# Two transformer blocks on one core: the filling matmuls of zeros taken out of TensorE's stream

## The chip, the cores and the metric

The kernel runs on one core of a Trainium2 chip. The metric is the device time of one execution in microseconds (us), of which the median of several runs is given; lower is better. The trace and the page come from one profiled execution.

## What is computed

256 tokens of width 1024 pass, in fp32, through three layers. The reference, cut to what matters here:

```python
# first block, two layers i = 0, 1
xn, mn = rms_norm(h, norm_mix[i]), rms_norm(mem, norm_mem[i])
# i = 0: forgetting attention, 12 heads of 64, causal, bias F[t] - F[s]
# i = 1: causal attention with ALiBi slopes, 12 heads of 64
# both: 4 more heads attend to 256 memory rows, without bias
h = h + heads @ w_out[i]
hn = rms_norm(h, norm_ffn[i])
h = h + (silu(gate) * up) @ w_down[i]
# second block, one layer
z = rms_norm(x) @ w_in
o_mla  = softmax(q @ k.T) @ v              # 16 heads, q and k 96 wide, v 64 wide
o_diff = (softmax(q1 @ k1.T) - lam * softmax(q2 @ k2.T)) @ v   # 8 heads, v 128 wide
x = x + (gate_a * o_mla + gate_b * norm(o_diff)) @ w_out
h2 = rms_norm(x)
affinity = softmax(h2 @ router_w)          # 16 experts
gate, idx = top_k(affinity per expert, 32) # each expert takes 32 tokens
y = (silu(xe @ w_gate) * (xe @ w_up)) @ w_down   # 1024 -> 2048 -> 1024 per expert
x = x + scatter_add(gate * y)
```

## The kernel before, in words

The program is written by hand, engine by engine: each engine has its own list of instructions in the order in which the code gives them, and the lists meet at semaphores (`wait_ge`, `then_inc`). Nothing reorders them, so an instruction on TensorE delays all that stand behind it there.

*Dense products.* Weights come in units of 1 MB into a ring in SBUF. ScalarE (L676) rounds a unit to its high part `wH`, VectorE (L1426) makes the low part `wL`, and TensorE multiplies high by high, high by low and low by high (`passes`, L992 to L994) into one PSUM sum. Activations are split the same way into `xH` and `xL`. This holds for the projections of both blocks, the output projections and the feed-forward loops.

*Norms.* A norm (`mem`, `mix0`, `ffn0`, `mix1`, `ffn1`, `attn`, `ffn2`, in this order) begins with squares on ScalarE (L699), a sum on VectorE, a root on ScalarE (L703) and the reciprocal, from which VectorE builds diagonal matrices (L1437). Then `transposes` on TensorE (L1014) multiplies the tokens by them and so turns and scales them at once; it waits for `norm_diag`. ScalarE and VectorE bring the result to SBUF, and the next dense product follows, column block by column block.

*Attentions.* There are four: `a0` and `a1` (layers 0 and 1 of the first block), `mla` and `dif` (second block). The first three have 32 maps (a head and a block of 128 queries each), two to a chunk, so 16 chunks; the width of a map is 128 or 256 keys for the causal heads, 256 for all others. TensorE's function `attention` goes round once per chunk: scores of chunk i (L1061, into banks 0 to 3), value products of chunk i-2 (L1075, 64 columns each), transposes of the probabilities of chunk i-1 (L1087). VectorE adds the bias (made by GpSimd, L605 and L609 in `a0`) and takes the row extreme (L1460, L1463), ScalarE takes the exponentials (L741), and VectorE copies the transposed probabilities to `pT_sb` (L1479), for which the value products wait. `dif` has a loop of its own with the same steps for 16 pairs of maps (L1313 scores, L1326 value products, L1336 transposes), in which VectorE mixes the two maps and ScalarE copies `pT_sb`. Behind each attention `turn_outputs` (L1101) transposes the outputs, and `out_proj` multiplies by the output weights.

*Matmuls of zeros.* `zeros` is a 128x512 bf16 tile, set once. `keep_busy(n, b)` (L999) issues n matmuls of it into bank b, 512 columns each; their result is never read, since the next matmul into that bank starts its sum anew. It is called:

- in `transposes`, ahead of the wait for the diagonal matrices: 30 for `attn`, 14 for `ffn0`, `mix1`, `ffn1`, `ffn2`;
- in `attention` and the loop of `dif`, behind the scores of the second and third iteration: 8 and 6 (`FILL`);
- in the same loops, ahead of the transposes of a chunk, from the third chunk on: 2 for `a0`, `mla` and `dif`, 1 for `a1` (`BUSY`), behind a wait for `att_pT`;
- 16 behind the loop of `dif`, and 18 in the choice of tokens, while VectorE looks for each expert's 32 best (L1831, L1833).

That is 86 + 56 + 98 + 34 = 274. Eight more matmuls of zeros at L1217 open the sums of the two feed-forward loops; they are not issued by `keep_busy`.

*Choice of tokens and experts.* The router product (L1129, 16 columns per matmul) is followed by a softmax, the search on VectorE, and matmuls by a 0/1 selection matrix (L1365). Then a loop over the 16 experts streams 24 MB of weights per expert through ten places of 1 MB; SyncE issues the transfers as places come free. The first places are filled while the attentions and the choice of tokens run.

Of the kernel before, what the change touches and what calls it, by code (L numbers as in the profile page):

```python
# [28 lines left out]
P = 128  # L29
# [33 lines left out]
def build(nc, x, mem, norm_mix, norm_mem, norm_ffn, norm_final, w_in_fox, b_fgate, w_in_moba,  # L63
# [4 lines left out]
    with ctx:  # L68
        def sb(name, shape, dt=F32):
            return ctx.enter_context(nc.sbuf_tensor(name, shape, dt))  # L70
# [5 lines left out]
        bank = [ctx.enter_context(nc.psum_tensor(f"bank{i}", [P, 512], F32)) for i in range(8)]  # L76

        def b2(i):
            return bank[i][:, :].rearrange("p (a n) -> p a n", a=2)
# [20 lines left out]
        zeros = sb("zeros", [P, 512], BF16)  # L100
# [122 lines left out]
        def diag(t):  # L223

            return pT_sb[:, t, 0, 0:P]
# [71 lines left out]
        def norm_at(name, k, v):  # L297

            before = NORMS.index(name) - (k == "dve")
            return before * ADDS[k] + v  # L300
# [65 lines left out]
        def width(kind, m):  # L366
            hd, qt = MAPS[m]
            return P * (qt + 1) if kind != "mla" and hd < NSELF else S

        def score_operands(kind, m):  # L370
            hd, qt = MAPS[m]
            if kind == "mla":
                return qTm[0:MLA_QK, hd, P * qt:P * qt + P], kTm[0:MLA_QK, hd, :]
            if hd < NSELF:
                return (kslice(qT, hd)[:, P * qt:P * qt + P], kslice(kT, hd)[:, 0:width(kind, m)])
            return kslice(qmT, hd - NSELF)[:, P * qt:P * qt + P], kslice(mkT[int(kind[1])], hd - NSELF)

        def value(kind, m, kt):
            hd, _ = MAPS[m]
            if kind == "mla":  # L380
                return v_mla[:, kt, HD * hd:HD * hd + HD]
            if hd < NSELF:
                return v_s[:, kt, HD * hd:HD * hd + HD]
            return v_m[int(kind[1])][:, kt, HD * (hd - NSELF):HD * (hd - NSELF) + HD]
# [36 lines left out]
        def _(sp):  # L421
# [32 lines left out]
            for n, (w, c0, _, _) in zip(mem_u[2:], MEMPROJ[2:]):  # L454
                load_cols(n, w, c0)
# [532 lines left out]
        def _(pe):  # L988
# [4 lines left out]
                pe.matmul(out, lh, rl, start=False, stop=False)  # L993
                return pe.matmul(out, ll, rh, start=False, stop=stop)  # L994

            def keep_busy(n, b):

                for _ in range(n):
                    pe.matmul(bank[b][:, :], zeros[:, 0:P], zeros[:, :], start=True, stop=True)  # L999

            def x_part(k, cols=slice(0, S)):
                return xH[:, k, cols], xL[:, k, cols]

            def transposes(name, src, first=4):

                n = nrm
                if name not in ("mem", "mix0"):
                    keep_busy(30 if name == "attn" else 14, 0)
                pe.wait_ge(n["diag"], norm_at(name, "diag", 2))
                for b in range(4):  # L1010
                    for j in range(2):
                        for t in range(NT):
                            k = 2 * b + j
                            mm = pe.matmul(b2(first + b)[:, j, P * t:P * t + P], src[:, t, P * k:P * k + P],  # L1014
                                           diag(t), start=True, stop=True)
                    mm.then_inc(n["tr"], 1)
# [29 lines left out]
                return [b2(b)[:, j, :] for j in range(2)]  # L1046


            BUSY = {"a0": 2, "a1": 1, "mla": 2, "dif": 2}

            FILL = (0, 8, 6)

            def attention(name, kind):
                base = att_base[name]
                for i in range(NMAP // 2 + 2):
                    if i < NMAP // 2:
                        if i >= 2:
                            pe.wait_ge(att["exp"], base["exp"] + 2 * i - 2)
                        for m in (2 * i, 2 * i + 1):
                            l, r = score_operands(kind, m)  # L1060
                            mm = pe.matmul(bank[m % 4][:, 0:width(kind, m)], l, r, start=True, stop=True)  # L1061
                        mm.then_inc(att["score"], 1)
                    if i < len(FILL):
                        keep_busy(FILL[i], 7)
                    if 0 <= i - 2 < NMAP // 2:
                        c = i - 2
                        g = c // 4
                        pe.wait_ge(att["pT"], base["pT"] + c + 1)
                        if c % 4 == 0 and g >= 2:
                            pe.wait_ge(att["o"], base["o"] + g - 1)  # L1070
                        for m in (2 * c, 2 * c + 1):
                            j = m % 8
                            nk = width(kind, m) // P
                            for kt in range(nk):
                                mm = pe.matmul(bank[6 + g % 2][:, HD * j:HD * j + HD],  # L1075
                                               pT_sb[:, c % 2, m % 2, P * kt:P * kt + P], value(kind, m, kt),
                                               start=(kt == 0), stop=(kt == nk - 1))
                        mm.then_inc(att["pv"], 1)
                    if 0 <= i - 1 < NMAP // 2:
                        c = i - 1  # L1080
                        if c >= 2:
                            pe.wait_ge(att["pT"], base["pT"] + c - 1)
                            keep_busy(BUSY[name], 4 + c % 2)
                        pe.wait_ge(att["exp"], base["exp"] + 2 * c + 2)
                        for m in (2 * c, 2 * c + 1):
                            for kt in range(width(kind, m) // P):
                                mm = pe.transpose(b2(4 + c % 2)[:, m % 2, P * kt:P * kt + P],  # L1087
                                                  p_sb[:, m % 4, P * kt:P * kt + P], ident[:, :])
                        mm.then_inc(att["tr"], 1)
# [55 lines left out]
            for L in range(2):  # L1145
                name = f"mix{L}"
# [10 lines left out]
                for u, (n, (_, _, how, _)) in enumerate(zip(proj_u[L], projections(L))):  # L1157
# [7 lines left out]
                    if L == 0 and u == 5:  # L1165
# [6 lines left out]
                        for i in range(6):  # L1172
                            if i >= 2:
                                pe.wait_ge(f_ev, i)
                            for j in range(2):
# [3 lines left out]
                                               start=True, stop=True)  # L1179
# [7 lines left out]
                name = f"ffn{L}"  # L1187
# [48 lines left out]
            for b in range(2):  # L1236
                for j in range(2):
                    for t in range(NT):
                        c = 2 * b + j
# [67 lines left out]
            for i in range(16 + 3):  # L1307
                if i < 16:
                    hd, qt = 4 * (i // 8) + i % 4, (i // 4) % 2
                    if i >= 2:  # L1310
                        pe.wait_ge(att["exp"], base["exp"] + 2 * i - 2)
                    for j in range(2):
                        mm = pe.matmul(bank[(2 * i + j) % 4][:, 0:S],  # L1313
                                       dqT[HD * j:HD * j + HD, hd, P * qt:P * qt + P],
                                       dkT[HD * j:HD * j + HD, hd, :], start=True, stop=True)
                    mm.then_inc(att["score"], 1)
                if i < len(FILL):
                    keep_busy(FILL[i], 7)
                if 0 <= i - 3 < 16:
                    n = i - 3  # L1320
                    hd, g, j = 4 * (n // 8) + n % 4, n // 4, n % 4
                    pe.wait_ge(att["pT"], base["pT"] + n + 1)
                    if j == 0 and g >= 2:
                        pe.wait_ge(att["o"], base["o"] + g - 1)
                    for kt in range(2):
                        mm = pe.matmul(bank[6 + g % 2][:, P * j:P * j + P], pT_sb[:, n % 2, 0, P * kt:P * kt + P],  # L1326
                                       v_d[:, kt, P * hd:P * hd + P], start=(kt == 0), stop=(kt == 1))
                    mm.then_inc(att["pv"], 1)
                if 0 <= i - 2 < 16:
                    n = i - 2  # L1330
                    if n >= 2:
                        pe.wait_ge(att["pT"], base["pT"] + n - 1)
                        keep_busy(BUSY["dif"], 4 + n % 2)
                    pe.wait_ge(dif_mix, n + 1)
                    for kt in range(2):
                        mm = pe.transpose(bank[4 + n % 2][:, P * kt:P * kt + P],  # L1336
                                          mix_sb[:, n % 2, P * kt:P * kt + P], ident[:, :])
                    mm.then_inc(att["tr"], 1)
            keep_busy(16, 4)
            turn_outputs("dif", 4, sn_mul)  # L1340
            out_proj(wout2_u, mTL, 0, 1)

# [8 lines left out]
            for t in range(NT):  # L1351
                mm = pe.transpose(bank[5][0:NE, P * t:P * t + P], aff[:, t, :], ident[:, :])
            mm.then_inc(ro_tr, 1)
            keep_busy(18, 7)
            pe.wait_ge(ro_key, 14)
            for t in range(NT):
                mm = pe.transpose(bank[6][:, NE * t:NE * t + NE], affT[:, 0, P * t:P * t + P], ident[0:NE, 0:NE])
# [4 lines left out]
            for k in range(KD):  # L1362
                for t in range(NT):
                    for part in (tokH, tokL):
                        mm = pe.matmul(bank[k][:, :], part[t][:, P * k:P * k + P],  # L1365
                                       sel[:, t].rearrange("p e c -> p (e c)"),
                                       start=(t == 0 and part is tokH), stop=(t == 1 and part is tokL))
# [3 lines left out]
            with pe.Fori(0, NE) as e:  # L1371
# [13 lines left out]
                for half in range(2):  # L1385
                    for k in range(KD):
                        w_ = arrived(8 * half + k)
                        for j in range(4):
                            mm = pe.matmul(bank[half][32 * j:32 * j + 32, :], xe[:, k, :],  # L1389
                                           w_[:, 512 * j:512 * j + 512],  # L1390
                                           start=(k == 0), stop=(k == KD - 1))
# [8 lines left out]
                for kc in range(16):  # L1400
                    if kc % 2 == 0:
                        w_ = rows_of(arrived(16 + kc // 2))
                    for q in range(4):
                        mm = pe.matmul(bank[3][32 * q:32 * q + 32, 0:256], hT[:, kc % 4, 32 * (kc // 4):32 * (kc // 4) + 32],  # L1404
                                       w_[:, kc % 2, 256 * q:256 * q + 256],
                                       start=(kc == 0), stop=(kc == 15))
# [490 lines left out]
```

## Time and profile before

| | us |
|---|---|
| median of 3 runs | 2052.25 |
| lowest and highest run | 2052.20, 2053.24 |
| span of the profiled execution, first to last instruction | 2051.5 |
| TensorE busy with matmuls | 1636.2 (80% of the span) |
| TensorE loading weights | 1064.7 (52%) |
| VectorE busy | 603.4 (29%) |
| ScalarE busy | 567.1 (28%) |
| GpSimd busy | 117.8 (6%) |
| mean granted clock of TensorE | 0.850 of full speed |
| read from HBM | 539.55 MB |

For the profiled execution the profile gives its span and no other time of its own; the runs' median lies 0.75 us above that span, which leaves that much for what lies around it. Busy times are shares of the whole span, an average over stages with different limits. The granted clock is what TensorE's throttle allowed: 1.0 is 2.4 GHz, 0.5 is 1.2 GHz, and a mean between them is a mixture of both.

### The profile page before, as it was taken

How to read it: one execution, taken by the hardware profiler on the slowest of the kernel's cores; microseconds unless marked ns; L12 is line 12 of the kernel's file. 1: busy time of each engine (PE TensorE's matmuls, PEld its weight loads, DVE VectorE, ACT ScalarE, POOL GpSimd, SP SyncE). 2: the span in 40 equal slices, each digit the busy share in tenths (PEclk: the TensorE clock that was granted, in tenths of full speed). 3: DMA queues.
4: the chain of work that ended last, by engine and by line, in shares of the span. 5: the costliest groups of instructions: out<-in, count | busy, mean ns of one | idle time of the engine just before them, and what ended most of it. 6: DMA issues, size and time to landing. Idle time of an engine off the chain costs nothing.

```text
span 2051.5 us, 27650 instructions
## 1 busy us (share of the span) xinstructions
PE 1636.2 (80%) x11433; PEld 1064.7 (52%) x11433; DVE 603.4 (29%) x867; ACT 567.1 (28%) x881; POOL 117.8 (6%) x167
## 2 busy tenths in 40 slices
PE   7999999999999998799887666666666666666666
PEld 6877999896899987789573111111111111111111
DVE  4344444545444445555752000000000000000000
ACT  6344344443543445625631000000000000000000
POOL 0040000002000003510100000000000000000000
PEclk9899999999999989999998677677677767776776
DMA  9421555450455523305144999999999999999998
GB/s 278 152 83 62 166 186 187 157 185 22 152 187 187 177 87 123 123 5 183 62 164 188 419 418 417 417 417 417 419 419 418 417 417 417 417 419 419 417 417 339
DMA packets 181999, 541.47 MB, mean 264 GB/s; under 512 B 12606, under 2 KB 106003, under 8 KB 149171
## 3 DMA queue, kind: packets, MB, share of 16 engines
q1 hardware_dynamic: 181890, 540.51, 68.8%
q8 instruction: 42, 0.69, 0.1%
q0 software_dynamic: 48, 0.13, 0.0%
q14 instruction: 19, 0.15, 0.0%
HBM read 539.55 MB, written 1.05 MB: 264 GB/s over the span
## 4 chain that ended last, share of the span: by engine, by line
PE 47%; DMA 37%; DVE 5%; ACT 4%; POOL 3%; SPq 2%; issue 2%; DVEq 0%; ACTq 0%; POOLq 0%
DMA ring<-in_expert_w_up_dram 17%; PE bank L992 11%; PE bank L993 11%; PE bank L994 11%; DMA arena<-in_expert_w_down_dram 10%; DMA ring<-in_expert_w_gate_dram 4%; PE bank L1389 4%; PE bank L1075 2%; PE bank L1129 1%; SPq L525 1%; DMA ring<-in_expert_w_down_dram 1%; PE bank L999 1%; DMA wide_L<-in_expert_w_up_dram 1%; DMA wide_H<-in_expert_w_down_dram 1%; DMA wide_L<-in_expert_w_gate_dram 1%
## 5 line engine op out<-in xcount | busy, mean ns | idle before, releaser
L1426 DVE TENSOR_TENSOR wL<-ring,wH 128x2048 fp32r<-128x2048 f32 x128 | 294.6, 2301 | 358.9 <-ACT wH L676 358.9
L676 ACT ACTIVATE wH<-ring 128x2048 fp32r<-128x2048 f32 x128 | 244.2, 1908 | 350.8 <-PE bank L994 349.2
L992 PE MATMUL bank<-xH,wH 128*128 128x256 f32 x1056 | 300.0, 284 | 4.4 <-DVE wL L1426 4.2
L993 PE MATMUL bank<-xL,wH 128*128 128x256 f32 x1056 | 298.8, 283 | 0.0
L994 PE MATMUL bank<-xH,wL 128*128 128x256 f32 x1056 | 298.7, 283 | 0.0
L1389 PE MATMUL bank<-ring,arena 128*32 128x512 f32 x1280 | 220.2, 812 | 71.8 <-DMA ring<-in_expert_w_up_dram 51.9
L992 PEld LDWEIGHTS bank<-xH,wH 128*128 128x128 f32 x1056 | 202.5, 192 | 6.7 <-issue 5.8
L993 PEld LDWEIGHTS bank<-xL,wH 128*128 128x128 f32 x1056 | 202.6, 192 | 0.8
L994 PEld LDWEIGHTS bank<-xH,wL 128*128 128x128 f32 x1056 | 202.6, 192 | 0.0
L1866 DVE TENSOR_TENSOR arena<-arena,bank 128x512 f32<-128x512 f32 x16 | 11.0, 688 | 541.4 <-PE bank L1389 541.4
L1389 PEld LDWEIGHTS bank<-ring,arena 128*32 128x32 f32 x1280 | 37.8, 132 | 244.2 <-DMA ring<-in_expert_w_up_dram 140.7
L1870 DVE TENSOR_TENSOR h<-h,bank 128x512 f32<-128x512 f32 x64 | 39.7, 682 | 348.6 <-PE bank L1413 348.6
L992 PE MATMUL bank<-wH,xH 128*128 128x256 f32 (+1 forms) x416 | 130.4, 313 | 2.5 <-DVE xL L1802 1.7
L993 PE MATMUL bank<-wL,xH 128*128 128x256 f32 (+1 forms) x416 | 129.5, 311 | 0.0
L994 PE MATMUL bank<-wH,xL 128*128 128x256 f32 (+1 forms) x416 | 129.4, 311 | 0.0
L980 ACT ACTIVATE arena<-bank 128x512 f32<-128x512 f32 x16 | 9.6, 597 | 329.3 <-PE bank L1396 329.3
L982 ACT ACTIVATE arena<-bank 128x256 f32<-128x256 f32 x16 | 6.1, 384 | 288.4 <-PE bank L1404 288.4
L992 PE MATMUL bank<-wH,hidH 128*128 128x512 f32 (+1 forms) x208 | 81.7, 393 | 5.2 <-DVE hidL L1677 2.0
L992 PEld LDWEIGHTS bank<-wH,xH 128*128 128x128 f32 x416 | 80.9, 195 | 7.5 <-issue 3.7
L994 PEld LDWEIGHTS bank<-wH,xL 128*128 128x128 f32 x416 | 80.8, 194 | 4.0
L993 PEld LDWEIGHTS bank<-wL,xH 128*128 128x128 f32 x416 | 80.8, 194 | 3.8
L993 PE MATMUL bank<-wL,hidH 128*128 128x512 f32 (+1 forms) x208 | 81.2, 391 | 0.0
(266 smaller groups left out, 2114.2 us busy)
## 6 DMA issues: line engine op xcount, KB each, us to landing
ring<-in_expert_w_gate_dram SPq DMA_DIRECT2D x96, 1024.0 KB, 19.2
ring<-in_expert_w_up_dram SPq DMA_DIRECT2D x64, 1024.0 KB, 24.2
ring<-in_w_gate_up_dram SPq DMA_DIRECT2D x44, 1024.0 KB, 5.1
arena<-in_expert_w_up_dram SPq DMA_DIRECT2D x32, 1024.0 KB, 26.0
ring<-in_expert_w_down_dram SPq DMA_DIRECT2D x32, 1024.0 KB, 27.3
wide_H<-in_expert_w_down_dram SPq DMA_DIRECT2D x32, 1024.0 KB, 20.5
wide_L<-in_expert_w_down_dram SPq DMA_DIRECT2D x32, 1024.0 KB, 18.8
arena<-in_expert_w_down_dram SPq DMA_DIRECT2D x32, 1024.0 KB, 18.7
```

What stands on the lines that cost most here:

```text
L525: sp.dma_start(dst, gv[e, u]).then_inc(landed, 16)
L676: act.activation(wH[:, n % 2, w], ring[:, slot(n), w], ACT.Copy).then_inc(w_hi, 1)
L992: pe.matmul(out, lh, rh, start=start, stop=False)
L993: pe.matmul(out, lh, rl, start=False, stop=False)
L994: return pe.matmul(out, ll, rh, start=False, stop=stop)
L999: pe.matmul(bank[b][:, :], zeros[:, 0:P], zeros[:, :], start=True, stop=True)
L1075: mm = pe.matmul(bank[6 + g % 2][:, HD * j:HD * j + HD], pT_sb[:, c % 2, m % 2, P * kt:P * kt + P], value(kind, m, kt), start=(kt == 0), s ...
L1129: mm = pe.matmul(out, l, r, start=(start and j == 0), stop=(stop and j == 1))
L1389: mm = pe.matmul(bank[half][32 * j:32 * j + 32, :], xe[:, k, :], w_[:, 512 * j:512 * j + 512], start=(k == 0), stop=(k == KD - 1))
L1426: dve.tensor_tensor(wL[:, n % 2, w], ring[:, slot(n), w], wH[:, n % 2, w].bitcast(F32), ALU.subtract).then_inc(w_split, 1)
L1866: dve.tensor_tensor(hid, sg, bank[1][:, :], ALU.mult).then_inc(e_hid, 1)
L1870: dve.tensor_tensor(hv, hv, b2(4 + q), ALU.add).then_inc(e_add, 1)
```

## The change

`keep_busy`, its tables `BUSY` and `FILL` and all of its calls are taken out; the waits around them stay. Nothing is put in their place. The tile `zeros` and the eight matmuls at L1217 remain.

```diff
@@
-            def keep_busy(n, b):
-
-                for _ in range(n):
-                    pe.matmul(bank[b][:, :], zeros[:, 0:P], zeros[:, :], start=True, stop=True)
-
@@ def transposes(name, src, first=4):
                 n = nrm
-                if name not in ("mem", "mix0"):
-                    keep_busy(30 if name == "attn" else 14, 0)
                 pe.wait_ge(n["diag"], norm_at(name, "diag", 2))
@@
-            BUSY = {"a0": 2, "a1": 1, "mla": 2, "dif": 2}
-
-            FILL = (0, 8, 6)
-
             def attention(name, kind):
@@
                         mm.then_inc(att["score"], 1)
-                    if i < len(FILL):
-                        keep_busy(FILL[i], 7)
@@
                             pe.wait_ge(att["pT"], base["pT"] + c - 1)
-                            keep_busy(BUSY[name], 4 + c % 2)
                         pe.wait_ge(att["exp"], base["exp"] + 2 * c + 2)
@@ the loop of dif
-                if i < len(FILL):
-                    keep_busy(FILL[i], 7)
@@
                         pe.wait_ge(att["pT"], base["pT"] + n - 1)
-                        keep_busy(BUSY["dif"], 4 + n % 2)
                     pe.wait_ge(dif_mix, n + 1)
@@
-            keep_busy(16, 4)
             turn_outputs("dif", 4, sn_mul)
@@ the choice of tokens
             mm.then_inc(ro_tr, 1)
-            keep_busy(18, 7)
             pe.wait_ge(ro_key, 14)
```

Because lines are taken out, L1014, L1061, L1075 and L1087 of before are L1007, L1050, L1062 and L1073 in the changed kernel. The order of instructions on VectorE, ScalarE, GpSimd and SyncE is the same in both.

TensorE in `a0`, one iteration with wide maps, before (`arena` holds queries, keys and values; `p_sb` the probabilities):

```order
L1061 MATMUL bank<-arena 128x256 [waits att_exp]
L1061 MATMUL bank<-arena 128x256
L1075 MATMUL bank<-arena,pT_sb 128x64 [waits att_pT]
L1075 MATMUL bank<-arena,pT_sb 128x64 x3
L999 MATMUL bank<-zeros 128x512 [waits att_pT]
L999 MATMUL bank<-zeros 128x512
L1087 MATMUL bank<-ident,p_sb 128x128 [waits att_exp]
L1087 MATMUL bank<-ident,p_sb 128x128 x3
```

The same iteration in the changed kernel:

```order
L1050 MATMUL bank<-arena 128x256 [waits att_exp]
L1050 MATMUL bank<-arena 128x256
L1062 MATMUL bank<-arena,pT_sb 128x64 [waits att_pT]
L1062 MATMUL bank<-arena,pT_sb 128x64 x3
L1073 MATMUL bank<-ident,p_sb 128x128 [waits att_exp,att_pT]
L1073 MATMUL bank<-ident,p_sb 128x128 x3
```

The transposes stand directly behind the value products, and the wait for `att_pT` has moved to them.

TensorE at the norm `ffn0`, between the output projection of `a0` and the first product of the feed-forward, before:

```order
L994 MATMUL bank<-wH,xL 128x512
L999 MATMUL bank<-zeros 128x512 x14
L1014 MATMUL bank<-pT_sb,h 128x128 [waits norm_diag]
L1014 MATMUL bank<-pT_sb,h 128x128 x15
L992 MATMUL bank<-xH,wH 128x256 [waits norm_dve,w_split]
```

And in the changed kernel:

```order
L994 MATMUL bank<-wH,xL 128x512
L1007 MATMUL bank<-pT_sb,h 128x128 [waits norm_diag]
L1007 MATMUL bank<-pT_sb,h 128x128 x15
L992 MATMUL bank<-xH,wH 128x256 [waits norm_dve,w_split]
```

Between the last product of the projection and the wait for the diagonal matrices nothing is left.

## Rows read from the trace of the kernel before

**Rows 1.** The page, part 2: granted clock of TensorE in 40 slices, in tenths.
```profile
PEclk9899999999999989999998677677677767776776
```

**Rows 2.** The chain that ended last, first expert: start us, us, what.
```profile
1118.70 18.81 DMA arena<-in_expert_w_down_dram
```

**Rows 3.** The tile `zeros`: matmuls, duration ns min/median/max, first and last start.
```profile
L999 PE MATMUL bank<-zeros x274: 377/379/634, 127.3 to 1088.2; 128*128 128x512 bf16 x137
```

**Rows 4.** The chain, a wide chunk of `a0`.
```profile
157.85 1.10 PE bank L1075 x8
158.96 0.43 PE bank L999 x2
159.39 0.45 PE bank L1087 x4
...
159.86 0.70 DVE pT_sb L1479
```

**Rows 5.** The attentions `a0`, `a1`, `mla`, `dif`: busy by engine, clock, DMA share, GB/s.
```profile
127.00:170.80 43.80, 39.28 (x258) 26.35 (x256) 24.12 (x81) 16.36 (x64) 26.68 (x44) 0.96 0.08 26
460.20:501.20 41.00, 36.80 (x248) 25.59 (x248) 24.24 (x81) 15.81 (x64) 14.35 (x20) 0.96 0.10 32
860.40:909.30 48.90, 46.48 (x298) 36.28 (x299) 26.08 (x56) 16.23 (x64) 0.00 (x0) 1.00 0.00 1
989.40:1030.00 40.60, 36.61 (x206) 21.69 (x207) 32.00 (x118) 24.48 (x85) 10.16 (x12) 0.94 0.05 21
```

In these rows the engines are, in order: TensorE's matmuls, its weight loads, VectorE, ScalarE, GpSimd.

**Rows 6.** The chain, GpSimd in `a0`.
```profile
139.84 0.46 POOL bias_sb L609
140.29 0.91 POOL bias_sb L605
```

**Rows 7.** The chain, `a1`: the first fill, and one matmul of zeros in a chunk.
```profile
460.89 3.01 PE bank L999 x8
...
476.58 0.22 PE bank L999
```

**Rows 8.** The chain, a chunk of `mla`.
```profile
874.34 1.02 PE bank L1075 x8
875.37 0.43 PE bank L999 x2
875.80 0.44 PE bank L1087 x4
876.23 0.87 PE bank L1061 x4
```

**Rows 9.** TensorE in time order, norms `ffn0` and `attn`; in brackets idle before and releaser.
```profile
196.08 3.20 PE L999 MATMUL bank<-zeros 128*128 128x512 bf16 x14
...
730.11 1.16 PE L1014 MATMUL bank<-pT_sb,h 128*128 128x128 f32 x8 [1.66 <-DVE pT_sb L1437]
```

**Rows 10.** The chain, the transposing matmuls of `ffn0`.
```profile
199.63 3.84 PE bank L1014 x32
```

**Rows 11.** Stretches with their granted clock (the columns of rows 5).
```profile
748.10:755.00 6.90, 6.90 (x35) 6.90 (x34) 2.04 (x6) 1.82 (x7) 0.00 (x0) 0.50 0.49 152
853.90:857.30 3.40, 3.40 (x18) 3.23 (x17) 0.00 (x0) 2.05 (x3) 3.40 (x2) 0.50 0.65 224
857.30:860.70 3.40, 2.16 (x18) 1.88 (x17) 0.00 (x0) 2.98 (x5) 2.06 (x1) 1.00 0.00 0
1034.80:1038.20 3.40, 1.64 (x12) 1.18 (x11) 2.67 (x5) 0.63 (x1) 0.00 (x0) 1.00 0.00 0
1038.20:1041.60 3.40, 3.40 (x9) 2.65 (x8) 2.63 (x5) 0.63 (x1) 0.00 (x0) 0.51 0.00 0
1080.00:1090.00 10.00, 7.33 (x28) 3.52 (x27) 6.54 (x22) 0.62 (x4) 0.00 (x0) 0.70 0.00 0
```

**Rows 12.** The chain: transposes of the heads ahead of `mla`, and the router product.
```profile
854.94 2.36 PE bank L1266 x11
...
1069.71 11.45 PE bank L1129 x64
```

## The prediction

> **What bounds the kernel now.** I read the slices of the page first, then the chain that ended last, then the four attentions and the norms one by one. The clock in 40 slices of 51 us [rows 1] shows two halves: 0.8 to 1.0 up to about 1100 us, where TensorE does dense work most of the time, and after that the loop over the experts, with the clock at 0.6 and 0.7 and no matmul of zeros in it; there the chain goes mostly through waits for weights, such as one of 18.81 us [rows 2]. All 274 matmuls of zeros [rows 3] lie between 127 and 1089 us, ahead of that loop. I take it that what the first half loses or gains moves the end by the same amount, since the DMA queues are at rest from 1080 to 1090 us, share 0.00 [rows 11]: the buffers are full by then, and that rest only gets longer or shorter.
>
> The matmuls of zeros cost 274 x 0.216 = 59 us of TensorE time (two take 0.43 us, [rows 4]). The question is how much of that is on the path, and what TensorE's clock does without them. The four attentions take 43.8, 41.0, 48.9 and 40.6 us at a mean clock of 0.96, 0.96, 1.00 and 0.94 [rows 5]; I call them a0, a1, mla and dif, as the code does.
>
> **What goes away, at an unchanged clock.**
> - a0: a wide chunk of two maps is a ring of 2.76 us in the chain [rows 4]: value products 1.10, two matmuls of zeros 0.43, four transposes 0.45, the copy on VectorE 0.70, and 0.08 between them. Without the zeros it is 2.33. For the first two thirds, though, the chain goes through GpSimd, which makes a bias in 0.91 + 0.46 + 0.07 = 1.44 us per map, 2.88 per wide chunk [rows 6]. GpSimd is late next there, and only the last 9 or so chunks can gain: at most 9 x 0.43 = 3.9; I take 3 us.
> - a1: one matmul of zeros a chunk, in the chain: 14 x 0.22 = 3.1 [rows 7]. Of the 14 that fill the first two iterations (8 took 3.01 us, 6 more 1.3 to 2.6) between 0 and 5 us are in the way; I take 2, since exponentials and a copy have to end in that time too. Together 5 us.
> - mla: TensorE alone makes the ring, 1.02 + 0.43 + 0.44 + 0.87 = 2.76 us [rows 8]. 14 x 0.43 = 6.0, and of the fills (14 x 0.216 = 3.0) half: 7.5 us.
> - dif: VectorE is busy 32.0 of 40.6 us [rows 5]. Between 0 and 9 us (14 x 0.43 and the fills); nearer the lower end, as another engine is nearly full: 3 us.
> - The norms (14 each before ffn0, mix1, ffn1 and ffn2, 30 before attn): TensorE still waits when the zeros are through; the 14 start 3.55 us ahead of the transposing matmuls and last 3.20, and behind the 30 it stands idle for 1.66 us [rows 9, 10]. Squares and root on ScalarE and VectorE hide all 86: nothing gained. The 16 behind dif and the 18 in the choice of tokens stand beside such chains of small steps too, and I take nothing for them (0 to 2 us).
>
> Sum at an unchanged clock: 3 + 5 + 7.5 + 3 = 18.5 us faster.
>
> **What the clock takes back.** TensorE's clock falls to the low level (0.5 granted, 1.2 GHz) after thin stretches and comes back after full ones. In the 3.4 us before 1038.2 it works 1.64 us, and the next stretch is low; behind that one, full of dense matmuls, it is high. In the low stretch from 853.9 it runs almost only transposes, without a gap, and from 857.3 it is high [rows 11]. It is not busy time alone: from 748.1 to 755.0 it is busy all 6.9 us, with thin matmuls of 32 columns (the part of the keys that is rotated), and stays low. At the low level 11 transposes take 2.36 us, 0.215 each [rows 12], against four in 0.45, 0.11 each, at the high one [rows 4].
>
> *Norms.* Without the zeros TensorE idles 3.55 us before 32 transposing matmuls of 3.84 us and a dense projection, where TensorE is the bound. The nearest row is the pause before 1038.2: one low stretch of 3.4 us behind it, in which dense work gets half done, 1.7 us lost. Bounds: 0 (nothing is lowered) and 3.4 (two such stretches). I take 1.7 for mix1, ffn0 and ffn1, and 2.0 for attn, whose pause becomes 6.5 + 1.66 = 8.1 us: 7 us. For ffn2 the thin matmuls of the router, 64 in 11.45 us [rows 12], are partly at the high level now: 0.11 and 0.215 each make 11.45 with about 22 at the high one, so up to 2.4 us more, and some for the transposing matmuls: 3, between 0 and 6.
>
> *Attentions.* Each starts with a pause of 2 to 3 us, and the fill in a1 itself ran at the low level, 3.01 / 8 = 0.38 us each [rows 7]. Without fills each of them begins low for longer. Does a chunk lift the clock by itself? At the low level a wide chunk of a0 or a1 is about 1.9 + 0.9 + 0.78 = 3.55 us. TensorE then has work almost throughout, yet much of it is products of 64 columns and scores on half the rows, so it lies between the thin matmuls of 748.1 (stay low) and the transposes of 853.9 (come back); nearer to the second, but only just. I expect the clock to swing. Against 2.76 now a low chunk costs 0.8 and a high one gains up to 0.43; in a1, against 2.54, it costs 1.0 and gains 0.21.
> - a0: all high -3, all low +8 (10 wide chunks at 0.8; narrow ones hide behind GpSimd). Two thirds low: +4.5.
> - a1: all high -5, all low +10. A little under half low: +1.5.
> - mla: has the most columns per chunk and no other engine in the ring. All high -7.5; all low, a chunk is 2 x (1.02 + 0.44 + 0.87) = 4.66, and 14 x (4.66 - 2.76) = +27. I take one low stretch at the start, then high: -6.
> - dif: all high -3, all low +4 (VectorE hides most of it): -0.5.
>
> The low level also reaches into the turning of the outputs and the output projection behind each attention, one more stretch at about two of the four places: +3 (0 to 6). The choice of tokens: +0.5 (0 to 2).
>
> **Sum**: +4.5 + 1.5 - 6 - 0.5 + 7 + 3 + 3 + 0.5 = +13 us. The profiled execution has a span of 2051.5; the median of the runs is 2052.25, 0.75 above it. So 2065 us.
>
> **The rivals.**
> 1. *Low throughout a0 and a1, high in mla.* For it: their products have few columns. Against it: TensorE would be busy almost without gaps. +8 and +10 for +4.5 and +1.5: 2065 + 12 = 2077. Chance 0.23.
> 2. *mla locked low too.* It hangs on the clock at which its first chunks run, since chunks at half speed deliver half the columns per us and keep it low. Against it: the stretch before mla has just brought the clock back [rows 11]. +27 for -6: 2098, or 2110 with rival 1. Chance 0.07.
> 3. *Transposes count for nothing with the clock.* Then a third of a chunk's TensorE time is no activity, and all four attentions stay low: +8 + 10 + 27 + 4 = +49 in place of -0.5, so 2115. The low stretch from 853.9 holds almost only transposes and the clock was back behind it [rows 11], so only 0.04. This is the rule of the Trainium skill, "TensorE: Matmul & The Clock Gate", Part 4, which says that a transpose on TensorE does not count as busy in the same way; the trace does not agree.
> 4. *Faster: the clock holds.* If a chunk of 2.33 us without zeros is dense enough from its third or fourth iteration on, the chains keep most of the 18.5 us, and norms and the rest give back some 9: 2052 - 18.5 + 9 = 2043. It decides when less than about a third of a0's wide chunks and a sixth of mla's are low (0.43 gained against 0.8 and 1.9 lost). For it: mla has a clock of 1.00 now. Chance 0.15.
> 5. *No change*, the gains in mla meeting the losses at the norms within 0.2% (4 us; less than that a measurement of this kernel cannot tell). Chance 0.10.
> 6. That the edit does nothing is excluded by the order on TensorE: no row of the helper is left. The 8 matmuls of zeros that open the sums of the feed-forward remain, outside the helper.
>
> The forecast keeps 0.41, with a range of its own of 2057 to 2073. For 8 in 10 the range reaches down to 2044, into the case that the clock holds, and up to 2098, the first form of rival 2. Slower by over 0.2%: 0.41 + 0.23 + 0.07 + 0.04 = 0.75; within it 0.10; faster 0.15.
>
> **What the profile after would show.** Each norm's 32 transposing matmuls at 5 us or more where they took 3.84, with a granted clock of 0.5 in or behind the pause; mla at 41 to 44 us with a clock over 0.9; a0 at 46 to 52 us with a clock of 0.6 to 0.8; dif as long as now; the loop over the experts as long as now. Wrong would be: a0 and a1 shorter than 43.8 and 41.0 us (rival 4), a clock of 0.5 throughout a0 and a1 (rival 1) or mla (rival 2), or a change of the loop that outweighs the first half.

## The result, and the profile after

The changed kernel takes 2084.23 us (median of 4 runs, 2083.75 to 2086.36) against 2052.45 us for the kernel before (4 runs, 2052.20 to 2053.24): 1.5% slower by the medians, and the ratio on record is 1.0159 with a 95% interval of 1.0145 to 1.0173. The forecast was 2065 us, slower by 13; it is slower by 32. Medians of different experiments were taken in different sessions, in which the kernel before had 2052.3 to 2053.2 us; the ratios compare within a session.

The profiled execution of the changed kernel has a span of 2082.0 us, 30.5 more than before. TensorE's clock in 40 slices, from the page (now 52 us each), which answers to [rows 1]:

```profile
PEclk9976999995799998899987767776776776677686
```

Two dips have appeared that were not there: slices 3 and 4 (104 to 208 us, tenths 7 and 6) and slices 10 and 11 (468 to 573 us, tenths 5 and 7). They are a0 and a1. The stretches that answer to [rows 5], with the same columns, a0, a1, mla and dif:

```profile
126.00:182.80 56.80, 52.58 (x220) 39.12 (x220) 24.83 (x81) 15.89 (x64) 26.66 (x44) 0.50 0.07 22
475.00:531.90 56.90, 52.08 (x220) 38.73 (x221) 24.80 (x81) 15.80 (x64) 14.33 (x20) 0.52 0.07 23
895.80:937.90 42.10, 38.88 (x257) 32.42 (x257) 26.09 (x56) 16.20 (x64) 0.00 (x0) 0.97 0.00 1
1019.80:1062.90 43.10, 30.46 (x161) 19.25 (x161) 34.80 (x124) 25.93 (x87) 10.14 (x12) 0.78 0.05 20
```

a0 ran at half clock from its first score to its last product. a1 began at the full clock, which fell 2.6 us in, in the pause behind the first scores, and then stayed low to the end:

```profile
475.00:477.60 2.60, 0.72 (x8) 0.52 (x8) 2.60 (x9) 0.52 (x3) 0.40 (x1) 1.00 0.25 87
477.60:531.90 54.30, 51.36 (x212) 38.20 (x213) 22.20 (x74) 15.28 (x62) 13.93 (x20) 0.50 0.06 20
```

mla ran at nearly the full clock, as expected, and is 6.9 us shorter. VectorE, ScalarE and GpSimd are busy about as long as before in the first three (24.83, 15.89 and 26.66 us in a0 against 24.12, 16.36 and 26.68).

The whole span by stage, worked out from the start of the first instruction of each stage in both traces (attentions from their first score to the first transpose of the outputs; norms belong to the stage behind them), in us:

| stage | before | after | difference |
|---|---|---|---|
| up to a0 | 126.5 | 126.0 | -0.5 |
| a0 | 44.3 | 56.9 | +12.6 |
| outputs of a0 | 28.8 | 29.3 | +0.5 |
| norm ffn0, feed-forward | 196.6 | 198.9 | +2.3 |
| norm mix1, projections | 64.0 | 64.0 | 0.0 |
| a1 | 41.0 | 56.9 | +15.9 |
| outputs of a1 | 27.6 | 29.0 | +1.4 |
| norm ffn1, feed-forward | 201.3 | 203.4 | +2.1 |
| norm attn, projections | 130.3 | 131.6 | +1.3 |
| mla | 48.9 | 42.0 | -6.9 |
| outputs of mla, projections | 80.1 | 82.0 | +1.9 |
| dif and the norm behind it | 44.6 | 43.1 | -1.5 |
| outputs of dif | 31.0 | 30.2 | -0.8 |
| norm ffn2, router, choice of tokens | 37.5 | 39.6 | +2.1 |
| loop over the experts | 949.1 | 949.3 | +0.2 |

Two wide chunks of a0 from the chain of the changed kernel, which answer to [rows 4] (L1050 scores, L1062 value products, L1073 transposes):

```profile
160.00 1.16 PE bank L1050 x4
161.16 1.90 PE bank L1062 x8
163.05 0.85 PE bank L1073 x4
163.91 1.16 PE bank L1050 x4
165.06 1.90 PE bank L1062 x8
166.96 0.85 PE bank L1073 x4
```

Such a chunk takes 1.16 + 1.90 + 0.85 = 3.91 us where it took 2.76. The copy on VectorE (0.70 us) has left the chain: it runs beside the scores, which take 1.16 us now, and TensorE alone makes the ring. That holds only where wide scores stand in the same round. Where they are narrow, or all issued already, the copy is still in the chain and a wide chunk takes 3.61 us; and a narrow chunk takes 1.04 + 0.43 + 1.16 = 2.63:

```profile
155.48 1.04 PE bank L1062 x4
156.52 0.43 PE bank L1073 x2
156.95 1.16 PE bank L1050 x4
...
176.41 1.97 PE bank L1062 x8
178.38 0.87 PE bank L1073 x4
...
179.27 0.70 DVE pT_sb L1460
```

From the starts of the value products of successive chunks in both traces, the 12.6 us of a0 and the 15.9 of a1 divide as follows (us):

| part | a0 before | a0 after | a1 before | a1 after |
|---|---|---|---|---|
| first score to first value product | 6.1 | 4.3 | 6.1 | 4.3 |
| six narrow chunks | 11.7 | 16.2 | 10.6 | 16.2 |
| ten wide chunks | 26.6 | 36.4 | 24.4 | 36.4 |

mla has no narrow chunks. Its chunk, which answers to [rows 8], has lost just its zeros, 1.02 + 0.44 + 0.87 = 2.33 us:

```profile
904.78 1.02 PE bank L1062 x8
905.80 0.44 PE bank L1073 x4
906.25 0.87 PE bank L1050 x4
```

The transposing matmuls of ffn0 and ffn2 ran at the low level; before it was 3.84 us for ffn0 [rows 10]. Those of ffn1 took 6.4 us and those of attn 5.5; those of mix1 stayed at 3.84, and no low stretch lies in the projections behind them. The router product behind ffn2 took 11.02 us against 11.45 [rows 12], so it did not get longer:

```profile
212.19 6.68 PE bank L1007 x32
```

```profile
1093.09 6.56 PE bank L1007 x32
1099.65 11.02 PE bank L1115 x64
```

### The profile page after: what moved, and what is told of

It reads as the page before. It is cut to its first block, busy times and chain, and to the rows that moved or that the text cites. A ratio compares the mean times of both kernels' runs of the same rounds, so it can differ in the third digit from the quotient of the medians.

```text
span 2082.0 us, 27158 instructions
## 1 busy us (share of the span) xinstructions
PE 1639.7 (79%) x11159; PEld 1086.9 (52%) x11159; DVE 605.7 (29%) x867; ACT 568.3 (27%) x881; POOL 118.1 (6%) x167
## 4 chain that ended last, share of the span: by engine, by line
PE 48%; DMA 37%; DVE 4%; SPq 4%; ACT 3%; POOL 2%; issue 2%; DVEq 0%; ACTq 0%; POOLq 0%
DMA ring<-in_expert_w_up_dram 19%; DMA ring<-in_expert_w_gate_dram 11%; PE bank L992 11%; PE bank L993 10%; PE bank L994 10%; DMA arena<-in_expert_w_down_dram 5%; PE bank L1062 3%; SPq L525 3%; PE bank L1370 2%; PE bank L1050 2%; PE bank L1007 2%; PE bank L1073 1%; PE bank L1115 1%; PE bank L1385 1%; DMA arena<-in_expert_w_up_dram 1%
## 5 line engine op out<-in xcount | busy, mean ns | idle before, releaser
L992 PEld LDWEIGHTS bank<-xH,wH 128*128 128x128 f32 x1056 | 203.4, 193 | 6.2 <-issue 5.2
L994 PEld LDWEIGHTS bank<-xH,wL 128*128 128x128 f32 x1056 | 203.4, 193 | 0.0
## 6 DMA issues: line engine op xcount, KB each, us to landing
arena<-in_expert_w_up_dram SPq DMA_DIRECT2D x32, 1024.0 KB, 26.6
```

What stands on the lines that cost most here:

```text
L992: pe.matmul(out, lh, rh, start=start, stop=False)
```

## Experiments

Kernels are named where a later expectation speaks of them. Two readings of a0 and a1 stood against each other. *The level latches*: a chunk without zeros is dense enough to hold the high level and too slow to leave the low one, so what counts is the level at its start. *Density alone*: without its zeros a chunk is too thin at either level. Besides, each stage's share of the loss was to be measured by itself.

### Zeros back in a0 and a1 alone

```diff
 changed kernel, plus
+ keep_busy(FILL[i], 7)                in attention, for a0 and a1 only
+ keep_busy({"a0": 2, "a1": 1}, ...)   ahead of the transposes of a chunk
```

> The changed kernel with the matmuls of zeros put back in a0 and a1 alone (fills 8 and 6, and 2 and 1 per chunk). The changed kernel had these two attentions at 56.8 and 56.9 us with a granted clock of 0.50 and 0.52, where they took 44.3 and 41.0 us before. If these two hold nearly all of the loss, they return to 44 and 41 us at a clock over 0.9, and the run takes 2084 - 28 = 2056 us (2053 to 2060). If the low clock there came from something else than the missing zeros of these stages (the norms' missing zeros, or the pauses ahead), a0 and a1 stay over 50 us and the run over 2070.

Measured: 2053.45 us (10 runs, 2048.71 to 2057.53), ratio to before 1.0007 (0.9993 to 1.0020). Its a0 and a1:

```profile
126.60:170.90 44.30, 39.21 (x258) 26.82 (x263) 24.58 (x81) 16.35 (x64) 26.64 (x44) 0.96 0.09 28
462.50:502.50 40.00, 35.05 (x243) 24.96 (x248) 24.25 (x81) 15.80 (x64) 14.32 (x20) 1.00 0.10 31
```

The clock is back in both and nearly the whole loss is gone: 2084.2 - 2053.5 = 30.8 us, of which 12.6 + 16.9 lie in the two attentions. For the other 204 missing matmuls of zeros, cost and gain are about equal.

### The fills alone

```diff
 changed kernel, plus
+ keep_busy(FILL[i], 7)                in attention, for a0 and a1 only
```

> The changed kernel with only the fills (8 and 6 matmuls of zeros) put back in a0 and a1, none per chunk. Theory L (the level latches): the clock stays as it begins, since at the high level a chunk takes 2.3 to 2.5 us and is dense, and at the low one 3.9 us and half as dense. a1, whose fills lift the clock, then holds it without zeros per chunk: 36 to 40 us at over 0.9. a0 has GpSimd's bias as its bound in narrow chunks, so TensorE pauses there, the clock may fall on the way and then stays low: 48 to 58 us. Run 2084 - 18 = 2066, between 2054 and 2072. Theory D (density alone): a chunk without its zeros is too thin at either level, so both fall within a few us of the fill and take 54 to 58 us: run 2082 to 2088.

Measured: median 2065.94 us of 10 runs, ratio to before 1.0046 (1.0025 to 1.0068), in two groups: four at 2052.92 to 2054.63, six at 2065.61 to 2067.66. The profiled execution is of the first group. In its trace, a0 up to 140 us, a0 from there, and the whole of a1:

```profile
126.40:140.00 13.60, 11.62 (x69) 7.00 (x71) 7.69 (x31) 5.81 (x24) 10.71 (x18) 0.87 0.26 89
140.00:181.80 41.80, 39.31 (x164) 30.20 (x164) 17.26 (x51) 10.42 (x40) 15.92 (x27) 0.50 0.00 1
472.30:509.60 37.30, 32.32 (x234) 23.08 (x235) 24.13 (x81) 15.78 (x64) 14.32 (x20) 0.99 0.10 33
```

a1 held the full clock for all but the last 0.8 of its 37.3 us without one matmul of zeros in a chunk. That speaks for the latch: the same chunks run at 0.52 in the changed kernel. a0 came up, fell at 140 us, in its first wide chunks, and never returned, and the run is in the shorter group all the same. Up to there GpSimd's bias stands in a0's chain (0.46 + 0.91 us per map), and its fourth chunk takes 3.14 us where a1's takes 1.89, so a0 is thinner; that this is why it fell is not shown. Which stage makes the second group 13 us longer is not settled; only one execution was profiled.

### One burst per attention

```diff
 changed kernel, plus, ahead of the transposes of a chunk
+ keep_busy(16 if c == 4 and name in ("a0", "a1") else 0, 4 + c % 2)
```

> The changed kernel with one burst of 16 matmuls of zeros in a0 and one in a1, ahead of the transposes of the fifth chunk, the first wide one; 32 of the 274 are back. Theory L (the level latches): the burst costs 3.5 to 7 us of TensorE's time, lifts the clock, and the wide chunks behind it hold it alone: a0 44 to 48 us, a1 39 to 45, run 2084 - 22 = 2062 (2055 to 2068). Theory D (density alone, or zeros needed in every chunk of a0): the clock falls again within two chunks, a0 and a1 stay at 57 us or more, run 2084 to 2092.

Measured: 2063.22 us (4 runs, 2062.37 to 2064.30), ratio to before 1.0052 (1.0035 to 1.0068), so 21 us less than the changed kernel, with 32 of 274 matmuls back. a0 and a1 take 46.3 us each. a0 ahead of the burst and behind it:

```profile
126.60:139.70 13.10, 11.01 (x48) 7.59 (x50) 7.01 (x29) 5.23 (x23) 10.32 (x17) 0.51 0.30 98
144.00:173.00 29.00, 24.70 (x179) 18.28 (x177) 17.25 (x52) 10.18 (x40) 12.29 (x22) 0.97 0.00 1
```

And the burst in the chain, with chunks behind it (here L1071 value products, L1083 transposes):

```profile
139.72 5.46 PE bank L999 x15
145.18 0.45 PE bank L1083 x4
...
146.39 1.10 PE bank L1071 x8
147.50 0.46 PE bank L1083 x4
147.98 0.70 DVE pT_sb L1471
...
148.72 1.10 PE bank L1071 x8
```

From 146.39 to 148.72 a chunk takes 2.33 us, the figure of the forecast for a chunk without zeros at the high level, and the 29 us behind the burst run at 0.97. Density alone is refuted: the same instructions run at 0.50 in the changed kernel and at 0.97 here, and what differs is the level at which they began. The 29 us include the ninth and tenth chunk, which are narrow, also without zeros.

The low level does not hold every loop, though. In the changed kernel dif began low as well (0.50 from 1020.3 to 1030.5 us) and came up without any matmul of zeros (1.00 from 1030.5 to 1043.1), so the latch is a finding on the chunks of a0 and a1. The rows of dif:

```profile
1020.30:1030.50 10.20, 9.19 (x36) 5.22 (x33) 8.08 (x32) 6.39 (x23) 4.21 (x5) 0.50 0.15 65
1030.50:1043.10 12.60, 9.65 (x64) 5.96 (x60) 11.77 (x45) 8.63 (x31) 5.09 (x6) 1.00 0.00 1
```

### Zeros out of mla alone

```diff
 kernel before, minus
- keep_busy(FILL[i], 7)                in attention, for mla only
- keep_busy(2, 4 + c % 2)              the same
```

> The kernel of before with the zeros of mla alone taken out (fills and 2 per chunk). In the changed kernel mla took 42.1 us at a clock of 0.97 against 48.9 before. If that gain is independent of the rest, this run is faster than before by 6.8 us: 2045.5 (2044 to 2048), with everything outside mla as before. If the high clock in mla was luck of the moment at which it starts, mla locks low here: a chunk of 4.6 us, mla at 70 to 77 us and the run at 2075 to 2082.

Measured: 2046.07 us (10 runs, 2042.85 to 2048.18), ratio 0.9970 (0.9960 to 0.9980), 6.2 us faster than before. mla takes 41.2 us for 48.9; the stage behind it gives 1.6 of the 7.7 us back (81.7 us for 80.1). The gain is independent of the rest, and in no profiled execution of any kernel here without zeros in mla did it lock low.

### Zeros back ahead of the norms alone

```diff
 changed kernel, plus
+ keep_busy(30 if name == "attn" else 14, 0)   in transposes
```

> The changed kernel with only the zeros ahead of the norms put back (86). If each norm lost some 2 us to a low clock behind its pause (the stretches from norm to norm grew by 2.3, -0.1, 2.1 and 1.2 us, and 1.7 at the router), this run is 5 to 8 us faster than the changed kernel: 2077 (2075 to 2080), with the 32 transposing matmuls of each norm at 3.84 us again. If those differences came from the attention ahead of them (a low clock carried over), the norms get nothing back and the run stays at 2083 to 2085.

Measured: 2075.38 us (4 runs, 2073.36 to 2078.00), 8.9 us less than the changed kernel. a0 stays as it was, so the low clock there has nothing to do with the norms:

```profile
127.50:184.30 56.80, 52.08 (x220) 38.72 (x220) 24.82 (x81) 15.88 (x64) 26.67 (x44) 0.51 0.07 21
```

The stages from ffn0 to mix1 and from ffn1 to attn take 196.5 and 201.3 us again, and the 32 transposing matmuls of every norm 3.84.

### Transposes in place of zeros

```diff
 kernel before, in the chunks of a0 and a1
- keep_busy(BUSY[name], 4 + c % 2)
+ 2 * BUSY[name] times pe.transpose(bank[4 + c % 2][:, 0:P], ident[:, :], ident[:, :])
```

> The kernel of before, in which each matmul of zeros inside the chunks of a0 and a1 is replaced by two transposes of the unit matrix (fp32, 128 columns), which take about the same time on TensorE (2 x 0.11 for 0.216 us). If transposes count with the clock as other matmuls do, as the stretch from 853.9 showed, all stays as before: a0 44 us, a1 41 us, run 2050 to 2056. If transposes do not count, the chunks are as thin as in the changed kernel: a0 falls and takes 56 to 60 us, run 2062 to 2085.

Measured: 2054.48 us (10 runs, 2051.12 to 2058.90), ratio 1.0010 (0.9999 to 1.0021), and a0:

```profile
128.20:172.60 44.40, 39.59 (x289) 29.85 (x290) 24.62 (x81) 16.36 (x64) 26.65 (x44) 0.96 0.10 30
```

So transposes of the unit matrix hold the clock in a0 as zeros do. The Trainium skill says in "TensorE: Matmul & The Clock Gate", Part 4, that transposes do not count as busy for the clock in the same way; here they count enough to keep a0 from falling, and the measurement decides. The next run shows how little is enough, so whether they count for as much as other matmuls stays open.

### Thin matmuls in place of zeros (busy_by_thin)

```diff
 kernel before, in the chunks of a0 and a1
- keep_busy(BUSY[name], 4 + c % 2)
+ 4 * BUSY[name] times pe.matmul(bank[4 + c % 2][:, 0:16], zeros[:, 0:P], zeros[:, 0:16], ...)
```

> The kernel of before, in which each matmul of zeros inside the chunks of a0 and a1 is replaced by four of 16 columns, whose weight loads keep TensorE as long (4 x 0.053 = 0.21 us). If the clock follows TensorE's busy time, all stays as before, run 2050 to 2056. If it follows what is streamed, a0's narrow chunks are as thin as without zeros: a0 falls to the low level and stays there, 56 us or more; a1, lifted by its fills, holds as it did with fills alone (37 to 41 us). Run 2062 to 2068.

Measured: 2052.68 us (10 runs, 2050.62 to 2054.66), ratio 0.9999 (0.9990 to 1.0009). The time is that of the first case of the expectation, but its premise was off: eight of them take 0.18 us in the chain, not 0.43. The second case, that a0 falls, did not come:

```profile
147.10 1.10 PE bank L1080 x8
148.20 0.18 PE bank L1004 x8
148.39 0.51 PE bank L1095 x4
```

```profile
127.70:171.00 43.30, 37.37 (x345) 27.49 (x346) 24.69 (x81) 16.36 (x64) 26.73 (x44) 0.94 0.10 31
```

So a0 needs far less than the zeros gave: these matmuls stream 128 columns a chunk where the zeros streamed 1024, and take less than half the time. Busy time alone is not what counts, since thin matmuls of another kind filled all of 748.1 to 755.0 in [rows 11] at the low level. These runs do not separate columns, number and time of the matmuls, and what a matmul counts with the clock stays open.

### The parts put together

The next four keep the zeros ahead of the norms and the fills in a0 and a1, and leave them out in mla, in dif, behind dif and in the choice of tokens. They differ in what a chunk of a0 and a1 gets:

```diff
 norms_a01:        keep_busy(2) in a0, keep_busy(1) in a1, as before
 a1_fill_alone:    keep_busy(2) in a0, nothing in a1
 parts_thin:       8 thin matmuls in a0, 4 in a1
 parts_thin_half:  4 thin matmuls in a0, 2 in a1
```

> A version from the parts: zeros kept ahead of the norms and in a0 and a1, taken out in mla, in dif, behind dif and in the choice of tokens. mla alone gave 6.2 us. dif took 44.6 us with zeros and 43 without, so 1 to 2 us more: 2052.3 - 6.2 - 1.5 = 2044.6 (2042 to 2047). If the zeros in or behind dif hold the clock for the output projection, it is 2 to 4 us slower than mla's alone: 2048 to 2050.

Measured: 2045.69 us (5 runs, 2044.40 to 2052.42), ratio 0.9973 (0.9956 to 0.9991). That is as mla alone; the 1 to 2 us of dif did not show.

> Zeros ahead of the norms, the fills in a0 and a1, and 2 per chunk in a0; none per chunk in a1, none in mla, in and behind dif and in the choice of tokens (against norms_a01 only a1's one per chunk is gone). With fills alone a1 took 37.3 us in the one execution that was profiled, but the ten runs of that kernel lay in two groups, 2053 to 2055 and 2066 to 2068. If a1 is what differed between them (it holds the high level in some executions and falls in others), this kernel's runs fall into two groups as well, near 2042 and near 2055. If a1 always holds and the second group came from a0 or mla, all runs are near 2045.7 - 3.7 = 2042.

Measured: 2045.38 us (7 runs, 2042.60 to 2047.06), ratio 0.9959 (0.9946 to 0.9973). One group, and a1 at 38.3 us:

```profile
461.90:500.20 38.30, 33.72 (x234) 23.72 (x235) 24.15 (x81) 15.78 (x64) 14.32 (x20) 0.96 0.10 33
```

No second group appeared in seven runs, so a1 very likely held in all of them (one was profiled), and a1's chunks by themselves do not make the two groups of the fills alone. But the kernel with the fills alone has no zeros ahead of mix1, the norm ahead of a1, and this one has, so a1 is not ruled out there. The 2.7 us gained in a1 do not show clearly in the median either (2045.38 against 2045.69, with runs 4 us apart).

> norms_a01 with each matmul of zeros inside the chunks of a0 and a1 replaced by four of 16 columns (8 and 4 per chunk). In busy_by_thin these took 0.18 us for eight in the chain instead of 0.43, and a0 and a1 were 1.0 us shorter each at a high clock. Theory: the gain adds up, 2045.7 - 2 = 2043.7 (2041.5 to 2045.5). If a0 held only by luck there, a0 falls here: 2055 or more.

Measured: 2042.71 us (5 runs, 2040.92 to 2044.86), ratio 0.9951 (0.9935 to 0.9967): 0.5% faster than before, which only a0's narrow chunks alone (below) equals; its median is the lowest here. The intervals of the versions without zeros in mla overlap, so their order is not shown. a0 42.7 us, a1 40.5.

> parts_thin with half as many thin matmuls per chunk, 4 in a0 and 2 in a1. If every matmul, however thin, counts with the clock by itself, half of them may be too few in a0's narrow chunks: a0 falls there and takes 55 us, run 2054 to 2057. If something else holds the clock in a0 (the place of the pauses), the count does not matter: run 2042 to 2045.

Measured: median 2056.29 us of 10 runs, ratio 0.9999 (0.9976 to 1.0022): two at 2038.69 and 2043.36, eight at 2055.40 to 2058.95. The profiled one is of the eight, and a0 in it behaves as with the fills alone:

```profile
128.20:142.00 13.80, 12.11 (x83) 7.58 (x84) 7.85 (x32) 5.78 (x24) 10.91 (x18) 0.88 0.28 93
142.00:185.80 43.80, 41.27 (x209) 32.17 (x209) 17.14 (x50) 10.43 (x40) 15.82 (x27) 0.50 0.00 0
```

The number of thin matmuls does matter. With four a chunk a0 stands on the edge: it fell in the run that was profiled, the other seven of its group are as long, and two of ten are as short as if it had held. A kernel that is near the edge does not get a little slower but 15 us slower, in some of its runs.

### a0's zeros in narrow chunks only

```diff
 norms_a01, ahead of the transposes of a chunk
- keep_busy(BUSY[name], 4 + c % 2)
+ keep_busy(0 if name == "a0" and not (c < 4 or c in (8, 9)) else BUSY[name], 4 + c % 2)
```

> norms_a01 with a0's zeros per chunk only where the maps are narrow (the third, fourth, ninth and tenth chunk); none in wide ones. The wide chunks behind the burst held the clock without zeros, at 2.33 us each. If the narrow chunks are the only place where a0 falls, a0 takes 41 to 43 us and the run 2045.7 - 2.5 = 2043 (2041 to 2045). If a0 also falls in the wide chunks in which GpSimd's bias is the bound (2.88 us a chunk instead of 2.33), it stays low from about the fifth chunk: a0 53 to 57 us, run 2054 to 2058.

Measured: 2044.05 us (5 runs, 2040.08 to 2045.87), ratio 0.9951 (0.9932 to 0.9969). a0:

```profile
127.40:170.30 42.90, 36.75 (x240) 26.09 (x242) 24.70 (x81) 16.35 (x64) 26.64 (x44) 0.90 0.10 30
131.00:165.00 34.00, 29.77 (x213) 21.21 (x212) 20.58 (x69) 14.78 (x57) 25.02 (x42) 1.00 0.09 30
165.00:170.30 5.30, 3.71 (x18) 3.12 (x16) 1.49 (x3) 0.00 (x0) 0.19 (x1) 0.51 0.00 0
```

The wide chunks of a0 held the full clock without zeros from 138 to 165 us, the first two of them at 2.88 us each, where GpSimd's bias is their bound. In the last two chunks, where TensorE has no scores left to issue, the clock fell: the last two periods before the turning of the outputs take 3.07 and 2.82 us where they took 2.75 and 1.96 in norms_a01. So what the zeros carry over is a0's first narrow chunks (the ninth and tenth held without them behind the burst) and its very end.

## Why the prediction was wrong in size

The sign and most terms hold, and 2084 lies in the wide range of 2044 to 2098, but not in the forecast's own of 2057 to 2073. Two terms carry all of the error. By the steps of the prediction:

- *Pass-through one to one.* Right: the loop over the experts took 949.3 us against 949.1.
- *mla: -6.* Right: -6.9, a chunk of 2.33 us and a clock of 0.97. The low stretch that was forecast for its start did not come; a short one came at its end.
- *Norms: +7, ffn2 and the choice of tokens: +3.5.* Right in sign, 7.8 us where 10.5 stood: +2.3, 0.0, +2.1 and +1.3 where 1.7, 1.7, 1.7 and 2.0 stood, and +2.1 where 3 + 0.5 stood. The router product, forecast to be up to 2.4 us longer, was 0.4 shorter. Given back their zeros, the norms returned 8.9 us. At mix1 the clock did not fall and nothing was lost, within the bounds of 0 to 3.4; why it did not fall there is open.
- *Outputs: +3.* +0.5 + 1.4 + 1.9 - 0.8 = +3.0. *dif: -0.5*: -1.5.
- *a0: +4.5.* Wrong: +12.6. *a1: +1.5.* Wrong: +15.9. These two miss by 22.5 us, more than the whole error of 17.5 in the span.

The step that failed first is "I expect the clock to swing", with two thirds of a0 low and a little under half of a1. It did not swing; it was low throughout, 0.50 and 0.52. Rival 1 had named this state and given it 0.23. The prediction compared a low chunk with two stretches of [rows 11] and called it "nearer to the second, but only just"; the burst and the fills alone show that in a1 and in the wide chunks of a0 the level that they begin at decides. What was held against rival 1, that TensorE would be busy almost without gaps, was true (52.58 of 56.8 us in a0) and did not bring the clock back. By the prediction's own prices this step is worth 8 + 10 in place of 4.5 + 1.5, so 12 of the 22.5 us.

The other 10.5 us are the price of the low level. Even all low, the prediction had +8 for a0 and +10 for a1, all of it in ten wide chunks. Its price of a low wide chunk was about 3.55 us (its terms 1.9 + 0.9 + 0.78 give 3.58), by doubling TensorE's part of the old chain and keeping VectorE's copy in it. That is nearly right where the copy stays in the chain (3.61) and too low where the scores take its place (3.91). Ten wide chunks cost 9.8 us more in a0 and 12.0 in a1. The larger miss is a term that was put at nothing, in a0 because "narrow ones hide behind GpSimd" and in a1 without a reason: the six narrow chunks cost 4.5 us in a0 and 5.6 in a1. The shorter start gave 1.75 us back in each. That is 9.8 + 4.5 - 1.75 = 12.6 and 12.0 + 5.6 - 1.75 = 15.9, to rounding.

So two steps failed, and the runs show both: the clock, which does not swing in these chunks but keeps its level, and the price of the low level, above all that of the narrow chunks. What in a chunk makes the low level hold is not shown. Rival 3, that transposes count for nothing, fell as expected: mla kept its clock.

## What to carry to other kernels

Before filler work is taken out of a loop, work out the loop's period at both levels of TensorE's clock, for each kind of round and with every step of TensorE in it, not only those on today's chain. The level that such a loop starts at may be the level it keeps (a0 and a1), or it may come up by itself (dif); only a run tells. Filler is worth it at the start and in the thin rounds (here the first narrow chunks, and ahead of the norms), and costs its full time where TensorE itself is the ring (mla, 6.2 us). A version that stands near the edge shows as two groups of runs, so time it often before it is trusted.

## What the runs showed of the hardware that was not expected

- One burst of 16 matmuls of 512 columns, in an attention of 46 us, decided the clock of the 29 us behind it (0.97 instead of 0.50).
- Matmuls of 16 columns on a stationary tile that does not change take 0.18 us for eight, and eight per chunk keep the high level in a0 (0.94) about as well as two matmuls of 512 columns (0.96); with four per chunk only two of ten runs are as short as if it had held.
- A loop can be busy on TensorE for 52.58 of 56.8 us and stay at the low level throughout (a0 in the changed kernel).
